# Two transformer blocks in one launch: a finer chain ahead of the experts, a reordered entry to block two, and turns of the identity in three pauses

## The chip, the cores and the metric

One core of a Trainium2 chip runs the whole kernel in one launch. The metric is the device time in microseconds (us), the median of three runs. PE is TensorE, DVE is VectorE, ACT is ScalarE, SP is the engine that issues the weight loads. All arithmetic is float32.

## The reference, cut to what matters

```python
x = x + gt1 * rmsnorm(y, g_post_mix)           # y = merged branches @ w_o, 256 tokens x 1024
h2 = rmsnorm(x, g_pre_ffn) * (1 + sc2) + sh2
logits = h2 @ w_router + b_router              # 32 experts
top_logits, top_e = lax.top_k(logits, 4)
top_w = softmax(top_logits)
gu = xe @ w_gu[e] + b_gu[e]                    # xe: the tokens of expert e
act = (clip(gu[:, D_FF:], -7, 7) + 1) * (min(gu[:, :D_FF], 7) * sigmoid(1.702 * ...))
yb = act @ w_dn[e] + b_dn[e]                   # added to the tokens, times top_w
x = x + gt2 * rmsnorm(f, g_post_ffn)           # f: the sum over a token's experts
# second block: h = rmsnorm(x, norm_mix_g_2); h @ w_in_2, gated linear attention, ...
```

## The kernel before, in words

The 256 tokens are two tiles of 128 (`tt`), each cut into two halves of 512 features (`h`); four such quarters make x. Each engine has one program written out by hand in the order in which it runs; semaphores (`wait_ge`, `then_inc`) join them. `step` on DVE waits until its own operation is done.

Weights stream through a ring of six slots of 2 MB. SP issues the load of a slot when PE has released it (`up_slot` for experts). An expert takes six slots, four for the up projection (`expert_item` on PE, L1830, products at L1839) and two for the down projection (L1876). For expert 0 the two down slots lie elsewhere (`first_down`), and slots 1, 2, 3 and then 0 are loaded during the merging and the `w_o` products; slot 0 last, once PE is done with the last `w_o` product. Expert 1's slots 4 and 5 are loaded ahead too, its slots 0 to 3 as PE releases them in item 0. From expert 2 on a loop loads each slot when the item before has released it. An item is an expert with up to 64 tokens; an expert with more has another item, with the same weights, for which nothing is loaded. There are 33 items here.

Ahead of the experts, for each tile: `w_o` products into PSUM banks `PB[0..3]` (`tokens`, L1551), ACT squares the halves and sums them (`square_half`, L742), DVE adds the two sums (`token_mean`, L1141), ACT takes the root (`token_root`, L748), DVE the reciprocal (`token_rstd`, L1147), scales the half with root and gain out of PSUM (`scale_y`, L1151) and adds it to x (`add_y`, L1156). ACT squares the new x, PE turns it (`turn_x`, L1733), ACT and for the last quarter DVE (L1185) copy the turned tiles, PE multiplies with the router weights (`router`, L1745), and DVE finds the four best experts (`top_experts`, L1163 to L1170). When both tiles are done PE makes ranks by a product with a triangle (L1765), DVE positions (L1190, L1192) and one hot matrices (L1198) of expert 0's tokens, PE gathers these tokens by a product with x (`gather`, L1807) and adds the up biases (`up_biases`, L1826), DVE copies the gathered rows (L1228), PE turns them (L1812), and DVE scales and shifts them (L1214, L1217) into `xe`, for which item 0's products at L1839 wait. During item 0 PE and DVE work out the overflow items (`overflow_counts`, `overflow_columns`), the first after slot 0, the second after slot 1.

After the last item PE adds the last outputs to the tokens (`combine`, L1818). Then ACT squares all four quarters, and DVE scales and adds (L1151, L1156), normalises for block two (`norm_half`, L1313), PE turns (`turn_normed`, L1908), ACT copies (L813), and PE starts block two with eight products of 512 columns for tile 0 (L1551), with the turns of tile 1 ahead of the seventh (`inside`). The low rank product (L1924) follows.

Of the kernel before, what the change touches and what calls it, by code (L numbers as in the profile page):

```python
# [24 lines left out]
P = 128  # L25
D = 1024
# [27 lines left out]
def layout(sizes):  # L54
# [10 lines left out]
    ("iota", P), ("cos", TT * DH), ("sin", TT * DH), ("carry", T), ("before32", NE), ("turn_id", 1), ("eps", 1),  # L65
# [11 lines left out]
def constants():  # L77
# [19 lines left out]
    put("iota", np.broadcast_to((p % CAP).astype(np.float32), (P, P)))  # L97
    nf = DH // 4
# [42 lines left out]
FOX_STEPS = 8  # L141


def two_blocks(nc, A, out):
    with ExitStack() as ctx:
# [272 lines left out]

        route_pe = sem("route_pe")
# [22 lines left out]
        moe_done = sem("moe_done")  # L442

# [144 lines left out]
        def _(act):  # L588
# [147 lines left out]
            def square_half(src):  # L736
# [5 lines left out]
                nc.scalar.activation([spare, spare_in, spare_mid, spare_final][0 if n < 8 else 1 if n < 16 else n // 4 - 2][n % 2], src, ACT.Square, scale=D ** -0.5, accum_out=part_ms[:, n:n + 1])\  # L742
                  .then_inc(part_sq, 1)

            def token_root(n):

                act.wait_ge(mean_ready, n + 1)
                nc.scalar.activation(tok_r[:, n:n + 1], mean_ms[:, n:n + 1], ACT.Sqrt, bias=C("eps"))\  # L748
                  .then_inc(tok_root, 1)
# [198 lines left out]
        def _(dve):  # L948
# [180 lines left out]
            V.memset(POSI, -FAR)  # L1129
# [8 lines left out]
            def token_mean(n):  # L1138

                dve.wait_ge(part_sq, 2 * n + 2)  # L1140
# [3 lines left out]
            def token_rstd(n):  # L1144

                dve.wait_ge(tok_root, n + 1)
# [12 lines left out]
            def top_experts(tt):  # L1159

                bank_ = [AS[1], AS[0]][tt]
                dve.wait_ge(logits_done, tt + 1)
                step(V.scalar_tensor_tensor(out=logit[:, tt, 0:NE], in0=bank_[:, 0:NE],  # L1163
# [6 lines left out]
                return V.tensor_tensor(sel[:, tt, :], mark[:, tt, 0:NE], logit[:, tt, 0:NE], ALU.is_gt)  # L1170

            dve.wait_ge(xtok_in, 16)
            dve.wait_ge(gain1_in, 16)
# [1020 lines left out]
```

## Time and profile before

| what | us |
|---|---|
| median of 3 runs (lowest, highest) | 1773.88 (1773.38, 1775.6) |
| the profiled execution's own time | 1777.78 |
| its span | 1776.0 |
| PE busy | 1685.5 (95%) |
| PE weight loads busy | 841.3 |
| DVE busy | 464.9 |
| ACT busy | 240.9 |
| products at L1839, 2112 of them | 472.1 |
| products at L1876, 1024 of them | 233.9 |
| expert loads, each 2 MB, 190 of them, issue to landing | 21.8 (median) |

The span is the profiled execution from its first to its last record; its own time holds what lies around it. Times in rows are from the start of the span. A busy PE is not PE at its peak. A row of the chain tells what the end of the program hung on at that time; PEclk is the granted TensorE clock as a share of 2.4 GHz.

### The profile page before, as it was taken

To read this page: it belongs to the slowest core of one execution; us is meant where nothing else is said; L and a number is where in the kernel's file an instruction comes from. 1 tells how busy PE (TensorE), PEld (TensorE's weight loads), DVE (VectorE), ACT (ScalarE), POOL (GpSimd) and SP (SyncE) were. 2 spreads that over 40 slices of the span, in tenths; PEclk is the share of its full clock that TensorE was granted. 3 is DMA by queue.
4 is the path that set the end of the run, shared out by engine and by line. 5 is a ranking of instruction groups with operands and counts; after the bars stand their busy time and mean duration, and the time that the engine had idled before them with its cause. 6 is when DMAs were issued, how large, how long until landed. Compare 5 with 4: busy or idle time off the path is not lost.

```text
span 1776.0 us, 19653 instructions
## 1 busy us (share of the span) xinstructions
PE 1685.5 (95%) x7790; PEld 841.3 (47%) x7791; DVE 464.9 (26%) x1031; ACT 240.9 (14%) x491; POOL 9.0 (1%) x5
## 2 busy tenths in 40 slices
PE   4999999899999999999999999999989999999998
PEld 2766677433333333332333333333344687588853
DVE  2303442421212212121212212121231623144411
ACT  2013440100000000000000000000131321100000
POOL 0010000000000000000000000000000000000000
PEclk9999999899999999999999999999989999999999
DMA  9652845569999999999799999999973232434400
GB/s 394 267 126 99 347 174 201 198 285 417 430 428 429 428 429 428 428 430 428 292 419 428 428 429 428 429 428 428 428 287 142 95 142 68 181 142 161 170 25 24
DMA packets 47841, 530.21 MB, mean 299 GB/s; under 512 B 13780, under 2 KB 13908, under 8 KB 15672
## 3 DMA queue, kind: packets, MB, share of 16 engines
q1 hardware_dynamic: 36720, 522.21, 71.0%
q10 hardware_dynamic: 11080, 7.42, 1.6%
q8 instruction: 30, 0.49, 0.1%
q14 instruction: 11, 0.09, 0.0%
HBM read 528.55 MB, written 1.06 MB: 298 GB/s over the span
## 4 chain that ended last, share of the span: by engine, by line
PE 71%; DMA 24%; DVE 3%; ACT 1%; issue 1%; SPq 0%; ACTq 0%; DVEq 0%
DMA ring<-experts_dram 23%; PE scores L1839 17%; PE proj L1551 10%; PE proj L2085 9%; PE att_out L1876 7%; PE proj L1541 6%; PE proj L2097 4%; PE proj L1668 3%; PE proj L1717 3%; PE turned L1807 2%; PE scores L1826 1%; PE scores L1633 1%; PE att_out L1657 1%; DMA rows<-rows_dram 1%; PE proj L1587 1%
## 5 line engine op out<-in xcount | busy, mean ns | idle before, releaser
L1839 PE MATMUL scores<-ring,arena 128*64 128x512 f32 x2112 | 472.1, 594 | 23.1 <-DMA ring<-experts_dram 19.8
L1839 PEld LDWEIGHTS scores<-ring,arena 128*64 128x64 f32 x2112 | 148.9, 137 | 333.1 <-issue 273.0
L1876 PE MATMUL att_out<-ring,arena 128*64 128x512 f32 x1024 | 233.9, 598 | 0.0
L1551 PE MATMUL proj<-ring,arena 128*128 128x512 f32 x384 | 170.1, 601 | 3.1 <-DVE arena L1116 2.5
L2085 PE MATMUL proj<-arena,ring 128*128 128x256 f32 x704 | 153.6, 382 | 0.7 <-ACT arena L813 0.7
L1290 DVE COPY arena<-turned 128x512 f32<-128x512 f32 x33 | 22.8, 692 | 480.4 <-PE turned L1807 480.4
L2085 PEld LDWEIGHTS proj<-arena,ring 128*128 128x128 f32 x704 | 134.7, 192 | 19.4 <-ACT arena L813 0.9
L1876 PEld LDWEIGHTS att_out<-ring,arena 128*64 128x64 f32 x1024 | 68.0, 136 | 140.9 <-issue 140.9
L1551 PEld LDWEIGHTS proj<-ring,arena 128*128 128x128 f32 x384 | 73.0, 192 | 92.1 <-issue 88.0
L1541 PE MATMUL proj<-arena,ring 128*128 128x256 f32 x512 | 113.1, 381 | 0.0
L1541 PEld LDWEIGHTS proj<-arena,ring 128*128 128x128 f32 x512 | 96.5, 190 | 14.9 <-issue 1.8
L793 ACT ACTIVATE arena<-arena 128x512 f32<-128x512 f32 x33 | 20.8, 629 | 556.1 <-DVE arena L1293 556.1
L2097 PE MATMUL proj<-ring,arena 128*128 128x512 f32 x176 | 75.7, 592 | 0.0
L1807 PE MATMUL turned<-xtok,arena 128*64 128x512 f32 x272 | 65.9, 606 | 0.7 <-DVE arena L1198 0.7
L1818 PE MATMUL proj<-arena 64*128 64x512 f32 x264 | 65.6, 615 | 0.8 <-ACT arena L802 0.8
L1204 DVE TENSOR_SCALAR arena<-cst,arena 128x128 f32<-128x128 f32 x68 | 20.5, 344 | 155.8 <-PE turned L1882 155.8
L1668 PE MATMUL proj<-arena,ring 128*128 128x256 f32 x256 | 59.5, 386 | 0.0
L1717 PE MATMUL proj<-arena,ring 128*128 128x256 f32 x256 | 55.8, 380 | 1.7 <-issue 1.0
L2097 PEld LDWEIGHTS proj<-ring,arena 128*128 128x128 f32 x176 | 33.4, 190 | 41.7 <-issue 41.6
L1717 PEld LDWEIGHTS proj<-arena,ring 128*128 128x128 f32 x256 | 48.5, 190 | 8.6 <-issue 1.2
L1668 PEld LDWEIGHTS proj<-arena,ring 128*128 128x128 f32 x256 | 47.3, 190 | 9.7 <-issue 3.9
L1293 DVE TENSOR_SCALAR arena<-scores 128x512 f32<-128x512 f32 x33 | 22.8, 692 | 90.4 <-PE scores L1839 90.4
(318 smaller groups left out, 1127.6 us busy)
## 6 DMA issues: line engine op xcount, KB each, us to landing
ring<-experts_dram SPq DMA_DIRECT2D x190, 2048.0 KB, 21.8
ring<-stream_dram SPq DMA_DIRECT2D x54, 2048.0 KB, 8.9
arena<-experts_dram SPq DMA_DIRECT2D x2, 2048.0 KB, 9.9
ring<-stream_dram SPq DMA_DIRECT2D x2, 1024.0 KB, 17.9
arena<-rpb_dram ACTq DMA_DIRECT2D x16, 128.0 KB, 4.3
arena<-gain_rows_dram ACTq DMA_DIRECT2D x3, 512.0 KB, 5.4
arena<-xT_dram SPq DMA_DIRECT2D x1, 1024.0 KB, 7.4
arena<-ctxT_dram SPq DMA_DIRECT2D x1, 1024.0 KB, 9.7
```

What stands on the lines that cost most here:

```text
L1290: V.tensor_copy(xg, PT[:, :]).then_inc(xg_ready, 1)
L1293: V.tensor_scalar(glu, AS[0][:, :], 7.0, None, ALU.min).then_inc(glu_ready, 1)
L1541: ins = mm(pb[:, c * T:c * T + T], W[:, k, (c0 + c) * P:(c0 + c) * P + P], src[:, k, :], start=k == 0, stop=k == K - 1)
L1551: ins = mm(pb[:, 0:n], src[:, k, tt * P:tt * P + P], W[:, k, 0:n], start=k == 0, stop=k == KD - 1)
L1668: ins = mm(PB[w % 2][:, 0:T], slot(n, KD, 512)[:, k, (w % 4) * P:(w % 4) * P + P], hT[:, k, :], start=k == 0, stop=k == KD - 1)
L1717: ins = mm(pb[:, c * T:c * T + T], slot(n, 4, D)[:, k, j * P:j * P + P], o[:, k, :], start=k == 0, stop=k == 3)
L1807: ins = mm(PT[parts, :], Sel[:, tt, :], xtok[:, tt, feats], start=tt == 0, stop=tt == TT - 1)
L1818: ins = mm(PB[2 * tt + h][:, :], SelWT[rows_, tile_of(tt)], yb[rows_, :], start=False, stop=False, skip_group_check=True)
L1839: ins = mm(AS[n][parts, :], xe[:, k % 4, k // 4, :], W[:, kk, n * D + feats.start:n * D + feats.stop], start=False, stop=k == KD - 1, skip ...
L1876: ins = mm(AO[parts, :], act_s[:, kk, s - 4, :], W[:, kk, feats], start=s == 4 and kk == 0, stop=s == 5 and kk == 3)
L2085: ins = mm(pb[:, c * T:c * T + T], W[:, k, c * 256 + j * P:c * 256 + j * P + P], hT[:, k, :], start=k == 0, stop=k == KD - 1)
L2097: ins = mm(PB[c][:, :], actT[:, 4 * n + k, tile_of(tt)], slot(DN0 + n, K, D)[:, k, half_of(h)], start=n == 0 and k == 0, stop=n == 5 and k ...
```

## The change

On the way to the experts: DVE multiplies a half of y with the gain while the root is not there yet, and a fused operation multiplies with the reciprocal and adds to x, in place of scale and add. The maxima are negated once for both tiles, after the one hots. `sel` of each tile is signalled by itself, the ranks of tile 0 are multiplied before `sel` of tile 1 is there, and a constant `iota_far` (128 columns more in `cst`) takes the offset of the positions, which are then one fused operation a tile. The gather of expert 0 works tile by tile into two banks with 256 columns each; DVE copies one and ACT the other, and `xe` is made in slices of 64 columns, half of them by ACT. Item 0's slot 0 waits for two of DVE's slices, slot 1 for ACT's, slot 2 for DVE's last. The up biases of item 0 stand ahead of the second router product, `overflow_counts` after slot 1 and `overflow_columns` after slot 2. The logits go to `PB[0]` and `PB[1]`, the ranks to `PB[2]` and `PB[3]`.

At the entry of block two: the same split into gain product and fused update, DVE and ACT taking tile 0's two banks in opposite order, tile 0's x squared and normed before tile 1's y is, and the first product waits for one copy instead of two. `PARTS` and `MEANS` give the new order of the sums.

`idle_turns` turns the identity matrix n times into a bank that nobody reads: 5 times after the first router product, 4 times between the rank products, 30 times after the last combine.

```diff
+    put("iota_far", np.broadcast_to((p % CAP + FAR + 1).astype(np.float32), (P, P)))
...
+PARTS = list(range(11)) + [12, 13, 11] + list(range(14, 24))
+MEANS = [0, 1, 2, 3, 4, 6, 5, 7, 8, 9, 10, 11]
...
-            act.wait_ge(top_ready, 1)
+            act.wait_ge(neg_max_ready, 1)
...
+            act.wait_ge(gathered, 1)
+            nc.scalar.activation(xg[:, 256:512], PB[0][:, 0:256], ACT.Copy).then_inc(xg_half, 1)
+            act.wait_ge(xg_t, 1)
+            for k in (2, 3, 6, 7):
+                ins = nc.scalar.activation(xe[:, k % 4, k // 4, :], PB[1][:, P * (k % 2) + CAP * (k // 4):][:, 0:CAP],
+                                           ACT.Identity, scale=A2[:, k:k + 1], bias=mod[:, 24 + k, 0:1])
+            ins.then_inc(xe_upper, 1)
...
-            for tt in range(TT):
-                act.wait_ge(moe_done, tt + 1)
-                for h in range(2):
-                    square_half(PB[2 * tt + h][:, :])
-                token_root(4 + tt)
-            for tt in range(TT):
-                square_of_x(4 + 2 * tt)
-                square_of_x(5 + 2 * tt)
-                token_root(6 + tt)
-                copy_normed(2 * tt, 0)
-                copy_normed(2 * tt + 1, 0)
+            act.wait_ge(moe_done, 1)
+            square_half(PB[0][:, :])
+            act.wait_ge(y_scaled, 1)
+            square_half(PB[1][:, :])
+            token_root(4)
+            act.wait_ge(moe_done, 2)
+            square_half(PB[2][:, :])
+            square_of_x(4)
+            square_of_x(5)
+            token_root(6)
+            square_half(PB[3][:, :])
+            copy_normed(0, 0)
+            copy_normed(1, 0)
+            token_root(5)
+            square_of_x(6)
+            square_of_x(7)
+            token_root(7)
+            copy_normed(2, 0)
+            copy_normed(3, 0)
...
-            def top_experts(tt):
...
+            def top_logits(tt):
...
-                step(V.scalar_tensor_tensor(out=logit[:, tt, 0:NE], in0=bank_[:, 0:NE],
+                step(V.scalar_tensor_tensor(out=logit[:, tt, 0:NE], in0=PB[tt][:, 0:NE],
...
-                V.tensor_scalar(nm1[:, tt:tt + 1], top8[:, tt, 0:1], -1.0, None, ALU.mult)
...
+            def top_experts(tt):
+                V.tensor_tensor(sel[:, tt, :], mark[:, tt, 0:NE], logit[:, tt, 0:NE], ALU.is_gt).then_inc(top_ready, 1)
+            def positions(tt):
+                dve.wait_ge(top_ready, tt + 1)
+                step(V.scalar_tensor_tensor(out=POSI[:, tt, 0:NE], in0=sel[:, tt, :], scalar=FAR,
+                                            in1=PB[2 + tt][:, 0:NE], op0=ALU.mult, op1=ALU.add))
+            def one_hot(tt, at):
+                return V.tensor_scalar(Sel[:, tt, :], C("iota_far")[:, 0:CAP], POSI[:, tt, at],
+                                       tok_r[:, 2 * tt + 1:2 * tt + 2], ALU.is_equal, ALU.mult)
...
+            expert_one_hot(slice(0, 1))
...
+                dve.wait_ge(part_sq, 4 * tt + 1)
+                V.tensor_tensor(scaled_mix[:, 0, :], PB[2 * tt][:, :], gain1[:, half_of(0)], ALU.mult)
                 token_mean(2 * tt)
+                step(V.tensor_tensor(scaled_mix[:, 1, :], PB[2 * tt + 1][:, :], gain1[:, half_of(1)], ALU.mult))
                 token_rstd(2 * tt)
...
-                    step(scale_y(tt, 2 * tt, gain1, h))
-                    add_y(tt, h, scaled_mix)
+                    V.scalar_tensor_tensor(out=xtok[:, tt, half_of(h)], in0=scaled_mix[:, h, :],
+                                           scalar=tok_r[:, 2 * tt:2 * tt + 1], in1=xtok[:, tt, half_of(h)],
+                                           op0=ALU.mult, op1=ALU.add).then_inc(x_half, 1)
                 if tt == 0:
+                    dve.wait_ge(x_half, 2)
                     token_mean(1)
                     token_rstd(1)
-            top_experts(0)
+            top_logits(0)
             dve.wait_ge(x_turned, 4)
...
+            top_experts(0)
             token_mean(3)
             token_rstd(3)
-            top_experts(1).then_inc(top_ready, 1)
-            dve.wait_ge(top_ready, 1)
-            step(V.tensor_scalar(mark[:, :, 0:NE], sel, FAR, -FAR - 1.0, ALU.mult, ALU.add))
+            top_logits(1)
+            top_experts(1)
+            dve.wait_ge(rank0_ready, 1)
+            positions(0)
+            one_hot(0, slice(0, 1)).then_inc(sel_first, 1)
             dve.wait_ge(route_pe, 1)
-            step(V.tensor_tensor(POSI[:, :, 0:NE], mark[:, :, 0:NE],
-                                 AS[1][:, 0:TT * NE].rearrange("p (t e) -> p t e", e=NE), ALU.add))
...
-                for tt in range(TT):
...
+            positions(1)
+            one_hot(1, slice(0, 1)).then_inc(sel_ready, 1)
+            V.tensor_scalar(nm1, top8[:, :, 0], -1.0, None, ALU.mult).then_inc(neg_max_ready, 1)
...
-            one_hots(slice(0, 1))
-            expert_one_hot(slice(0, 1))
+            dve.wait_ge(gathered, 1)
+            V.tensor_copy(xg[:, 0:256], PT[:, 0:256]).then_inc(xg_ready, 1)
+            dve.wait_ge(xg_half_t, 1)
+            for k in (0, 1, 4, 5):
+                ins = V.tensor_scalar(xe[:, k % 4, k // 4, :], AO[:, P * (k % 4) + CAP * (k // 4):][:, 0:CAP],
+                                      A2[:, k:k + 1], mod[:, 24 + k, 0:1], ALU.mult, ALU.add)
+                if k == 1:
+                    ins.then_inc(xe_lower, 1)
+            ins.then_inc(xe_ready, 1)
...
-            dve.wait_ge(gathered, 1)
-            V.tensor_copy(xg, PT[:, :]).then_inc(xg_ready, 1)
...
-            dve.wait_ge(xg_t, 1)
-            expert_input(step)
...
-                step(V.tensor_copy(n_e, PB[0][0:NE, 0:1]))
+                step(V.tensor_copy(n_e, PB[2][0:NE, 0:1]))
...
+            def gain_y(tt, h):
+                return V.tensor_tensor(scaled_ffn[:, h, :], PB[2 * tt + h][:, :], gain2[:, half_of(h)], ALU.mult)
+            def update_x(tt, h):
+                V.scalar_tensor_tensor(out=xtok[:, tt, half_of(h)], in0=scaled_ffn[:, h, :],
+                                       scalar=tok_r[:, 4 + tt:5 + tt], in1=xtok[:, tt, half_of(h)],
+                                       op0=ALU.mult, op1=ALU.add).then_inc(x_half, 1)
+            dve.wait_ge(moe_done, 1)
+            gain_y(0, 1).then_inc(y_scaled, 1)
+            dve.wait_ge(part_sq, 9)
+            step(gain_y(0, 0))
             token_mean(4)
             token_rstd(4)
-            step(scale_y(0, 4, gain2, 0))
-            token_mean(5)
-            add_y(0, 0)
-            step(scale_y(0, 4, gain2, 1))
-            add_y(0, 1)
-            token_rstd(5)
-            step(scale_y(1, 5, gain2, 0))
+            update_x(0, 0)
+            update_x(0, 1)
+            dve.wait_ge(x_half, 6)
+            dve.wait_ge(part_sq, 11)
+            gain_y(1, 0)
             token_mean(6)
-            step(scale_y(1, 5, gain2, 1))
             token_rstd(6)
...
-            for h in range(2):
-                add_y(1, h)
+            dve.wait_ge(part_sq, 14)
+            step(gain_y(1, 1))
+            token_mean(5)
+            token_rstd(5)
+            update_x(1, 0)
+            update_x(1, 1)
             token_mean(7)
             token_rstd(7)
...
             turn_x(1)
...
             router(0)
+            idle_turns(AS[0], 5)
             turn_x(2)
             turn_x(3)
+            pe.wait_ge(ohb_ready, 1)
+            pe.wait_ge(bgu_in, 48)
+            up_biases()
             router(1)
             pe.wait_ge(top_ready, 1)
-            for tt in range(TT):
-                for s in range(tt + 1):
-                    ins = mm(AS[1][:, tt * NE:tt * NE + NE], tri[:, s, tt * P:tt * P + P], sel[:, s, :],
-                             start=s == 0, stop=s == tt)
-            ins.then_inc(route_pe, 1)
-            mm(PB[0][0:NE, 0:1], sel[:, 0, :], ones[:, 0:1], start=True, stop=False).then_inc(up_slot, RING)
-            mm(PB[0][0:NE, 0:1], sel[:, 1, :], ones[:, 0:1], start=False, stop=True).then_inc(route_pe, 1)
+            mm(PB[2][:, 0:NE], tri[:, 0, 0:P], sel[:, 0, :], start=True, stop=True).then_inc(rank0_ready, 1)
+            mm(PB[3][:, 0:NE], tri[:, 0, P:2 * P], sel[:, 0, :], start=True, stop=False)
+            idle_turns(PB[0], 4)
+            pe.wait_ge(top_ready, 2)
+            mm(PB[3][:, 0:NE], tri[:, 1, P:2 * P], sel[:, 1, :], start=False, stop=True).then_inc(route_pe, 1)
...
-                mm(PB[0][0:NE, 1:2], C("before32")[0:NE, :], eblk[:, 2:3], start=True, stop=True).then_inc(route_pe, 1)
+                mm(PB[2][0:NE, 1:2], C("before32")[0:NE, :], eblk[:, 2:3], start=True, stop=True).then_inc(route_pe, 1)
...
-            halves = [(slice(CAP * b, CAP * b + CAP), slice(512 * b, 512 * b + 512)) for b in range(2)]
+            def gather_first(tt):
+                for q, bank_ in enumerate((PT, PB[0])):
+                    for parts, feats in halves:
+                        ins = mm(bank_[parts, 0:256], Sel[:, tt, :],
+                                 xtok[:, tt, feats.start + 256 * q:feats.start + 256 * q + 256], start=tt == 0,
+                                 stop=tt == TT - 1)
+                return ins
...
-                pe.wait_ge(xe_ready, i + 1)
+                if not first:
+                    pe.wait_ge(xe_ready, i + 1)
...
+                    if first and s == 0:
+                        pe.wait_ge(xe_lower, 1)
+                    if first and s == 1:
+                        pe.wait_ge(xe_upper, 1)
+                    if first and s == 2:
+                        pe.wait_ge(xe_ready, 1)
...
-                    if first and s == 0:
+                    if first and s == 1:
...
-                    if first and s == 1:
+                    if first and s == 2:
...
+            pe.wait_ge(sel_first, 1)
+            gather_first(0)
             pe.wait_ge(sel_ready, 1)
-            gather()
-            pe.wait_ge(ohb_ready, 1)
-            pe.wait_ge(bgu_in, 48)
-            up_biases()
-            pe.wait_ge(xg_ready, 1)
-            turn(AO, xg).then_inc(xg_t, 1)
+            gather_first(1).then_inc(gathered, 1)
+            mm(PB[2][0:NE, 0:1], sel[:, 0, :], ones[:, 0:1], start=True, stop=False).then_inc(up_slot, RING)
+            mm(PB[2][0:NE, 0:1], sel[:, 1, :], ones[:, 0:1], start=False, stop=True).then_inc(route_pe, 1)
+            for c in range(4):
+                if c == 0:
+                    pe.wait_ge(xg_ready, 1)
+                if c == 2:
+                    pe.wait_ge(xg_half, 1)
+                ins = nc.tensor.transpose([AO, PB[1]][c // 2][:, c % 2 * P:c % 2 * P + P], xg[:, c * P:c * P + P], ident)
+                if c == 1:
+                    ins.then_inc(xg_half_t, 1)
+            ins.then_inc(xg_t, 1)
...
+            idle_turns(AS[0], 30)
...
-            pe.wait_ge(hT_ready, 2)
+            pe.wait_ge(hT_ready, 1)
...
-            tokens(slot(0, KD, 512), hT, 0, inside=lambda: [turn_normed(hn1, c, 0) for c in (2, 3)])
+            tokens(slot(0, KD, 512), hT, 0, inside={4: lambda: pe.wait_ge(hT_ready, 2),
+                                                    6: lambda: [turn_normed(hn1, c, 0) for c in (2, 3)]})
...
+            def idle_turns(bank_, n):
+                for _ in range(n):
+                    nc.tensor.transpose(bank_[:, 0:P], ident, ident)
```

## Rows read from the trace of the kernel before

**Rows 1.** The page, part 2: busy tenths in 40 slices of the span.
```profile
PE   4999999899999999999999999999989999999998
...
DMA  9652845569999999999799999999973232434400
```

**Rows 2.** Chain that ended last, experts: start us, us, what.
```profile
379.26 10.30 PE scores L1839 x48
...
406.83 10.30 PE scores L1839 x48
...
582.94 25.48 DMA ring<-experts_dram
```

**Rows 3.** Windows before item 0: stretch, length, busy of each engine, PEclk, DMA share, GB/s.
```profile
330.00:332.00 2.00, 2.00 (x12) 2.00 (x11) 0.51 (x3) 1.59 (x3) 0.00 (x0) 0.50 0.31 131
...
334.00:336.00 2.00, 1.79 (x10) 1.65 (x10) 0.53 (x3) 0.53 (x2) 0.00 (x0) 0.50 0.00 0
```

**Rows 4.** Timeline of SP's queue after item 0's first slot: start us, us.
```profile
347.99 69.66 SPq L531 DMA_DIRECT2D ring<-experts_dram  x13
```

**Rows 5.** Windows, columns as in rows 3: the three stretches at the lower clock.
```profile
328.00:342.00 14.00, 11.55 (x46) 6.96 (x46) 6.62 (x31) 3.38 (x8) 0.00 (x0) 0.51 0.19 81
...
366.00:372.50 6.50, 6.50 (x21) 1.83 (x21) 0.76 (x2) 0.60 (x1) 0.00 (x0) 0.50 0.68 290
...
1298.00:1308.00 10.00, 7.08 (x14) 3.75 (x15) 5.76 (x13) 3.23 (x10) 0.00 (x0) 0.50 1.01 430
```

**Rows 6.** Timeline: start us, us, engine, line, operation, [idle before <-releaser], ahead of the experts.
```profile
323.81 1.87 PE L1745 MATMUL scores<-arena 128*128 128x32 f32 x16
...
324.79 0.16 DVE L1141 TENSOR_TENSOR small<-small 128x1 f32<-128x1 f32 x1 [9.52 <-ACT arena L742]
...
325.52 0.75 DVE L1151 SCALAR_TENSOR_TENSOR arena<-proj,small,arena 128x512 f32<-128x512 f32 x1
...
327.05 0.66 PE L1733 MATMUL turned<-cst,xtok 128*128 128x128 f32 x4 [1.38 <-DVE xtok L1156]
...
329.35 3.46 PE L1745 MATMUL scores<-arena 128*128 128x32 f32 x16
329.59 0.69 DVE L1185 COPY arena<-att_out 128x512 f32<-128x512 f32 x1
...
334.15 0.53 ACT L787 ACTIVATE arena<-arena,small 128x32 f32<-128x32 f32 x2 [1.96 <-DVE arena L1170]
...
334.17 1.49 PE L1765 MATMUL scores<-arena,cst 128*128 128x32 f32 x6 [1.36 <-DVE arena L1170]
...
336.62 3.68 PE L1807 MATMUL turned<-xtok,arena 128*64 128x512 f32 x8 [0.65 <-DVE arena L1198]
...
340.23 1.96 PE L1826 MATMUL scores<-arena 64*64 64x512 f32 x8
...
342.82 0.69 DVE L1214 TENSOR_TENSOR arena<-att_out,small 128x512 f32<-128x512 f32 x1 [1.27 <-PE att_out L1812]
...
344.29 3.65 PE L1839 MATMUL scores<-ring,arena 128*64 128x512 f32 x16 [1.51 <-DVE arena L1217]
...
357.36 1.89 PE L1807 MATMUL turned<-xtok,arena 128*64 128x512 f32 x8
```

**Rows 7.** Timeline, as rows 6: PE at the entry of block two.
```profile
1291.02 1.99 PE L1818 MATMUL proj<-arena 64*128 64x512 f32 x8 [0.79 <-ACT arena L802]
...
1300.23 1.11 PE L1908 MATMUL turned<-cst,arena 128*128 128x128 f32 x4 [7.23 <-DVE arena L1313]
...
1302.89 7.95 PE L1551 MATMUL proj<-ring,arena 128*128 128x512 f32 x12 [0.69 <-ACT arena L813]
...
1313.36 1.07 PE L1924 MATMUL turned<-arena 128*32 128x256 f32 x16
```

**Rows 8.** Chain that ended last, its first piece.
```profile
1.65 15.57 DMA rows<-rows_dram
```

**Rows 9.** DMA issues: what, queue, KB, us to landing.
```profile
cst<-cst_dram ACTq DMA_DIRECT2D x1, 849.5 KB, 7.6
```

More of the change, by code:

```diff
@@ L417, in two_blocks @@
         hT_ready = sem("normed_half_copied")
+        neg_max_ready = sem("negated_maxima_ready")
+        rank0_ready = sem("first_token_ranks_ready")
+        sel_first = sem("first_token_sel_ready")
+        xg_half = sem("gathered_upper_columns_copied")
+        xg_half_t = sem("gathered_lower_columns_turned")
+        xe_lower = sem("first_xe_lower_tiles_ready")
+        xe_upper = sem("first_xe_upper_tiles_ready")
         route_pe = sem("route_pe")
@@ L741, in square_half @@
                     act.wait_ge(part_sq, n - 1)
-                nc.scalar.activation([spare, spare_in, spare_mid, spare_final][0 if n < 8 else 1 if n < 16 else n // 4 - 2][n % 2], src, ACT.Square, scale=D ** -0.5, accum_out=part_ms[:, n:n + 1])\
+                scratch = [spare, spare_in, spare_mid, spare_final][0 if n < 8 else 1 if n < 16 else n // 4 - 2][n % 2]
+                nc.scalar.activation(scratch, src, ACT.Square, scale=D ** -0.5,
+                                     accum_out=part_ms[:, PARTS[n]:PARTS[n] + 1])\
                   .then_inc(part_sq, 1)
             def token_root(n):
-                act.wait_ge(mean_ready, n + 1)
+                act.wait_ge(mean_ready, MEANS.index(n) + 1)
                 nc.scalar.activation(tok_r[:, n:n + 1], mean_ms[:, n:n + 1], ACT.Sqrt, bias=C("eps"))\
@@ L1246, in overflow_items @@
                 lo, begin, end = eblk[:, 3:4], eblk[:, 4:5], eblk[:, 5:6]
-                step(V.tensor_tensor(lo, PB[0][0:NE, 1:2], C("turn_id")[0:NE, :], ALU.add))
+                step(V.tensor_tensor(lo, PB[2][0:NE, 1:2], C("turn_id")[0:NE, :], ALU.add))
                 step(V.tensor_tensor(begin, lo, ident[0:NE, 0:1], ALU.subtract))
@@ L1543, in features, with tokens @@
                 ins.then_inc(state[1], 1)
-            def tokens(W, src, tt, n=512, inside=None):
+            def tokens(W, src, tt, n=512, inside={}):
                 pb = bank()
                 for k in range(KD):
-                    if inside is not None and k == 6:
-                        inside()
+                    if k in inside:
+                        inside[k]()
                     ins = mm(pb[:, 0:n], src[:, k, tt * P:tt * P + P], W[:, k, 0:n], start=k == 0, stop=k == KD - 1)
@@ L1744, in router, with up_biases @@
                         pe.wait_ge(xT_ready_b, 1)
-                    ins = mm([AS[1], AS[0]][tt][:, 0:NE], hT[:, k, tile_of(tt)], wr2[:, k, :], start=k == 0,
+                    ins = mm(PB[tt][:, 0:NE], hT[:, k, tile_of(tt)], wr2[:, k, :], start=k == 0,
                              stop=k == KD - 1)
                 ins.then_inc(logits_done, 1)
+            halves = [(slice(CAP * b, CAP * b + CAP), slice(512 * b, 512 * b + 512)) for b in range(2)]
+            def up_biases():
+                for parts, feats in halves:
+                    for n in range(2):
+                        rows_ = slice(64 * n, 64 * n + 64)
+                        ins = mm(AS[n][parts, :], OHb[rows_, :], bgu[rows_, feats], start=True, stop=False,
+                                 skip_group_check=True)
+                ins.then_inc(bias_added, 1)
             pe.wait_ge(merged_ready, KD)
@@ L2073, in _ @@
             tokens(slot(12, KD, 512), merged2, 1)
-            tokens(slot(13, KD, 512), merged2, 1, inside=lambda: [turn_normed(hn2, c, 4) for c in (0, 1)])
+            tokens(slot(13, KD, 512), merged2, 1, inside={6: lambda: [turn_normed(hn2, c, 4) for c in (0, 1)]})
             turn_normed(hn2, 2, 4)
```

34 lines of the change are left out of this document (13 added, 21 removed).

## The prediction

> **What bounds the kernel now.** I read the page's forty slices first (44.4 us each), then the chain that ended last, then the timelines of the two stretches that the diff touches, then the granted clock. PE is busy in nearly every slice; DMA is full from the tenth to the twenty-ninth, about 400 to 1290 [rows 1]. The chain [rows 2] shows how the two take turns. An expert item costs PE 27.6 us (379.26 to 406.83). From 582.94 the chain goes over the load of expert weights: 25.48 us of DMA, then 3.7 to 3.9 of PE, about 29.4 us an item. So most of the span can't be shortened by PE or DVE. But a load is issued only when PE releases a ring slot, and the stream has no head start: the DMA engines are idle at 334 to 336 [rows 3], and SP issues expert 1's slot 0 at 347.99, just after PE has used slot 0 for the first time (344.29 plus 3.65) [rows 4, 6]. The whole stream of loads is hung on the start of the first item. What item 0 starts earlier, everything up to 1291 ends earlier, DMA bound or not.
>
> The path touched is thus (a) from the last `w_o` product (to 323.8) to item 0's first product at 344.29, and (b) from the last combine at 1291.02 to block two's first product at 1302.89 and on to 1313.36, where the low rank product starts. In both PE waits for DVE and ACT, and in both the granted clock falls to its lower level (1.2 of 2.4 GHz): 328 to 342 and 1298 to 1308, mean 0.51 and 0.50 [rows 5].
>
> **Part a, step by step.** *x update.* Before, after the square sum (324.79 plus 0.16) come root, reciprocal, a 0.75 us scale out of PSUM and an add, which at 512 columns is 0.69; PE turns the quarter at 327.05, in 0.66 [rows 6]. Now the gain product (0.7, by the same row) runs beside ACT's root, and one fused 0.7 us operation follows: 324.95 + 0.75 + 0.25 + 0.7 = 326.65, and the last quarter 0.7 later, 327.35, against 328.38. Gain 0.35 and 1.0. *Copy and second router.* DVE drops one operation and moves two, so its copy of 512 columns starts at 328.3 instead of 329.59 and ends at 329.0. PE fills the time with the four up bias products, off the path from now on. Router 1 starts at about 328.9; the second half's copy holds it little. It took 3.46 us with the clock low, router 0 took 1.87 with it high [rows 6]. End 330.8 (high) or 332.4 (low), against 332.81.
>
> *Ranks.* From the router's end (332.81) to the first use of `sel` (ACT, 334.15) it is 1.3 us [rows 6], now 1.2 with one operation fewer: `sel` at 332.0. PE has done all but one of the three rank products; each is 0.5 low (1.49 for three) or 0.25 high. Four turns take 0.43 at 0.11 each and end at 331.8, before `sel`. Last rank 332.35. Positions fall from two DVE operations and a wait to one fused one (0.22), and token half 0 has position and one hot while PE is at the rank: `sel_first` 332.6, `sel_ready` 333.2. *Gather.* 3.68 us low, 1.89 high for the same operation [rows 6]. Half 0 starts at 332.65; in all it ends at 334.4, against 340.3. *Copy, turns, input.* Before: up biases (1.96) and beside them the 0.69 copy, then turns, then two operations on 512 columns from 342.82, and the product at 344.29 [rows 6]. Now DVE and ACT copy 256 columns each (half of 0.69, with the fixed part 0.4), two turns, and DVE makes two 64 column slices (about 0.2 each) before PE may begin: 334.5 + 0.4 + 0.35 + 0.45 = 335.7, say 335.8. ACT's four slices, about 0.25 each, end by 336.6 and slot 1 wants them only at 339.2; ACT's exponentials before them (0.53 [rows 6]) end by 334.0. Total for (a): 344.3 - 335.8 = **8.5 us gained** with the clock high. New operations here have no row of their own; bounds from the nearest: a PSUM slice of 64 columns between 0.15 and 0.35, the same for ACT, so the start lies between 335.4 and 336.6.
>
> Cover. Expert 0's slot 0 must have landed: SP issues it when PE ends the last `w_o` product, and DMA moves its last bytes between 330 and 332 [rows 3]; 335.8 leaves 4 us. Item 0's inner work is the same; the expert counts and the overflow columns move one slot later in PE's order, which gives DVE 3.4 us more for each, so I cost them at nothing; if DVE were later than that, PE would stand in item 0 with slots landed.
>
> **The clock.** Part (a) costs at the low level: router +1.6, ranks +0.4, gather +1.8, turns +0.2, less 0.5 that hides beside DVE: 3.5 us. So with a low clock (a) gains 5.0. The five, four and thirty turns are there for this. At 5 x 0.11 the first fill 325.7 to 326.2, at no cost, since PE waits until 326.65.
>
> **Part b.** Before: the four squares and the two x updates in series; first normed half at 1300.2, turned, copied, product at 1302.89 after both copies [rows 7]. Now: square of half 0 from 1292.2, DVE takes half 1's gain product meanwhile, then half 0's; second square ends at 1293.6, mean, root, reciprocal 0.8: 1294.4; two fused 0.7: 1295.1, 1295.8; squares of x to 1296.7 (they now follow the updates directly, 0.7 apart); mean, root, reciprocal 0.75; normed half 0.75: PE turns at 1298.25 against 1300.23 [rows 7]. First product after one copy: 1298.25 + 0.45 + 0.65 = 1299.35 against 1302.89. Then six of eight steps (5.15 at 0.86 a step), the turns of the second token half, for which DVE is ready at 1304.5 and 1305.15 (0.3 late), 1.7 for the last two: 1307.3. The row of before for the same point is 1313.36. **Gain 6.0 us** with the clock high. Thirty turns are 3.3 us, 1293.0 to 1296.3, at no cost before 1298.25; at the low clock they would be 6.4 and late by 1. Weights of block two's slot 0 land before 1299 either way: the stream fills six slots in turn and its first has landed by the first product already today [rows 7]. With the clock low (b) loses 2.8 on the product (twelve records took 7.95 against 5.16) and 0.2 on turns: it gains 3.0.
>
> **Part c.** The constants grow by 128 columns, 64 KB on 849.5, on the ACT queue ahead of `rows`, with which the chain opens (15.57 us) [rows 8, 9]. At 131 to 430 GB/s, the rates in [rows 3, 5], this is 0.15 to 0.5; if the chain's opening waits for `rows` alone and its packets don't queue behind, 0. I take **0.3 lost**.
>
> **Does a turn of the identity hold the clock?** The trace cannot decide it: no stretch of before is filled by turns alone. It shows that it fell at 1298 after 5 us of nothing, at 328 after short pauses among turns and 32 column products, and that it stayed low from 1298 to 1308 although turns lay in it, from 1300.23 [rows 5, 7]. The last speaks a little against turns. The Trainium skill, TensorE: Matmul & The Clock Gate, Part 4: PE-mode transpose, says that the full clock doesn't engage for transposes, since they don't count as busy in the same way. By that rule this case would come out as the first rival; the trace agrees only in that the turns from 1300.23 didn't raise it.
>
> **Sum.** Against the profiled execution (span 1776.0, own time 1777.78): +0.3 - 8.5 - 6.0, and +1.0 since even held by turns the clock will fall in some executions: -13.2, 1764.6. The median of the runs is 3.9 below that execution, which gives 1760.7. Nothing shows what the 3.9 is; as part of it may be clock that the timed runs did not lose and can't win back, I add a third of it, 1.3: **1762.0 us**. A further low stretch, 366 to 372.5 in item 0, at mean 0.50 [rows 5], costs some 3 us of PE time; it begins in 32 row bias products that the diff leaves as they are, and may stay or go: 3 us either way in a single execution.
>
> **Rivals.** *Turns don't hold the clock.* +0.3 - 5.0 - 3.0 = -7.7: 1777.8 - 7.7 - 3.9 = **1766.2**. For it: turns that raised nothing. Against it: the pauses themselves get shorter. *Part (a) is swallowed by the expert stream*, only (b) stays: 1777.8 + 0.3 - 6.0 - 3.9 = **1768.2**. Against it: idle DMA before 348. *The edits do less than they say*, because the finer pieces each pay for their handing over: some 30 new waits at 0.1 and slices at 0.35 instead of 0.2 take 4 us, the clock another 7, **1770 to 1774**. *Slower:* the pauses in finer pieces let the clock fall late, near 334, and item 0, with its bias products of 32 rows, never raises it before item 1. Its some 30 us of PE work at half speed would cost 27: 1762 + 27 = **1789**; it decides from 12 us of PE work beyond today's at the low level. Against it: today the clock is low from 328 to 342 and no longer, at a longer pause [rows 5].
>
> **Chances.** Forecast 0.50; turns without effect 0.38; swallowed 0.05; less than said 0.04; slower 0.03. A measurement here tells 0.2% (3.5 us) from nothing. The first three are faster by more: 0.93; within 0.04; slower 0.03. The two likely cases with 3 us of item 0's clock and the slices' bounds reach from 1757.5 to 1768.5.
>
> **What would show it.** Item 0's first expert product at 335 to 337, and SP's load of expert 1 slot 0 3.7 us later; gather near 1.8 us; the granted clock 1.00 from 325 to 345 and from 1293 to 1310; item 1 again at 27.6 us and a 29.4 us rhythm in the DMA stretch, shifted as a whole; the low rank product 16.3 us after the last combine starts, against 22.3. Wrong if the clock is low in either stretch, if the first product waits for ACT's slices or a load, or if the shift at item 1 isn't found at 1291.

## The result, and the profile after

The changed kernel's median is 1762.95 us (6 runs, 1759.59 to 1766.7) against 1774.74 (6 runs, 1772.73 to 1778.85): 11.8 us faster, ratio 0.9931 (95% interval 0.9915 to 0.9946). (The three runs of the table above are among these six.) Its profiled execution took 1762.79, with a span of 1760.9. The page, part 2, for [rows 1]:

```profile
PE   4999999999999999999999999999999999999998
...
DMA  9642845779999999999799999999974232344400
```

Nothing is to be seen there: PE is at 90% or more in all slices but the first and the last; before, two more stood at 8. The change shows in the timeline, ahead of the experts, for [rows 6]:

```profile
325.30 1.87 PE L1816 MATMUL proj<-arena 128*128 128x32 f32 x16
...
327.01 0.74 PE L1744 MATMUL scores<-cst 128*128 128x128 f32 x5
327.02 0.16 DVE L1175 RECIPROCAL small<-small 128x1 f32<-128x1 f32 x1
327.22 1.42 DVE L1231 SCALAR_TENSOR_TENSOR xtok<-arena,small,xtok 128x512 f32<-128x512 f32 x2
...
328.02 0.66 PE L1804 MATMUL turned<-cst,xtok 128*128 128x128 f32 x4 [0.27 <-DVE xtok L1231]
...
329.27 1.09 PE L1826 MATMUL scores<-arena 64*64 64x512 f32 x8
...
330.29 1.97 PE L1816 MATMUL proj<-arena 128*128 128x32 f32 x16
...
333.56 0.41 PE L1852 MATMUL proj<-arena,cst 128*128 128x32 f32 x2 [0.38 <-DVE arena L1199]
...
334.01 0.65 PE L1888 MATMUL turned<-xtok,arena 128*64 128x256 f32 x4
...
336.96 1.10 DVE L1272 TENSOR_SCALAR arena<-att_out,small 128x64 f32<-128x64 f32 x4 [0.53 <-PE att_out L1984]
337.18 1.29 ACT L806 ACTIVATE arena<-proj,small 128x64 f32<-128x64 f32 x4 [0.79 <-PE proj L1984]
337.61 7.09 PE L1927 MATMUL scores<-ring,arena 128*64 128x512 f32 x32 [0.47 <-DVE arena L1272]
```

Router 1 takes 1.97 us where it took 3.46; the first expert product follows 12.31 us after router 0's start, where it took 20.48; slots 0 and 1 run in one piece of 7.09 without waiting for ACT's slices. SP issues expert 1's slot 0 at 341.31, 3.70 after that product's start, as before. The same for the entry of block two, PE alone, for [rows 7]:

```profile
1280.22 1.99 PE L1907 MATMUL proj<-arena 64*128 64x512 f32 x8 [0.79 <-ACT arena L822]
...
1282.14 3.49 PE L1744 MATMUL scores<-cst 128*128 128x128 f32 x30
...
1287.45 0.66 PE L2005 MATMUL turned<-cst,arena 128*128 128x128 f32 x4 [1.82 <-DVE arena L1364]
...
1288.80 5.42 PE L1617 MATMUL proj<-ring,arena 128*128 128x512 f32 x12
...
1296.74 1.07 PE L2022 MATMUL turned<-arena 128*32 128x256 f32 x16
```

Twelve records in 5.42 instead of 7.95. The windows over both places and over item 0 (stretch, length, busy of each engine, PEclk, DMA share, GB/s) answer to [rows 5]:

```profile
326.00:342.00 16.00, 14.52 (x104) 8.73 (x105) 10.32 (x45) 6.39 (x18) 0.00 (x0) 1.00 0.36 133
355.00:374.00 19.00, 19.00 (x88) 6.70 (x86) 5.38 (x12) 2.21 (x4) 0.00 (x0) 1.00 0.44 174
1280.00:1296.00 16.00, 13.93 (x69) 8.66 (x70) 9.64 (x21) 8.71 (x25) 0.00 (x0) 1.00 1.01 431
```

The clock is at its higher level throughout all three. The next table divides the profiled executions of both kernels and of the experiments by the starts of PE's records, in us. "Start" runs from the big modulation product near 42 us to router 0, "item 0" from its first product to item 1's first, "stream" from there to the last combine, "entry" on to the low rank product, "rest" to the end of the span:

| kernel | start | router 0 to first expert product | item 0 | stream | entry | rest |
|---|---|---|---|---|---|---|
| before | 281.76 | 20.48 | 34.80 | 911.93 | 22.34 | 462.64 |
| changed | 283.28 | 12.31 | 31.58 | 911.03 | 16.52 | 464.16 |
| no_turns | 283.02 | 13.64 | 33.16 | 911.67 | 19.11 | 464.18 |
| turns_only | 283.32 | 19.20 | 31.57 | 911.35 | 22.12 | 462.57 |
| entry_only | 282.94 | 19.02 | 31.57 | 911.54 | 16.52 | 463.82 |
| chain_only | 281.76 | 12.31 | 33.16 | 909.50 | 21.64 | 464.19 |
| long_turns | 281.83 | 13.72 | 34.80 | 911.76 | 36.31 | 464.38 |
| biases_back | 283.15 | 12.01 | 31.58 | 911.52 | 16.52 | 464.06 |
| more_turns | 280.27 | 12.31 | 31.57 | 910.56 | 16.52 | 461.24 |
| spread_more | 280.27 | 12.31 | 32.74 | 911.14 | 18.22 | 461.29 |
| spread_before | 281.81 | 20.50 | 32.74 | 910.84 | 22.22 | 464.18 |
| dve_alone | 281.70 | 12.30 | 33.16 | 912.55 | 18.21 | 464.19 |

From before to changed: 8.2 us in the chain, 3.2 in item 0, 0.9 in the stream, 5.8 at the entry; 1.5 and 1.5 are lost at the start and in the rest. Sum 15.1, the difference of the spans. (Products, and the changed kernel run once more, divide as the changed kernel does, within 0.3 us but for the stream, which is 0.6 shorter in the second.)

The profiled execution of before is one of its slower ones, so this overstates the change. turns_only below is the kernel before with turns that brought no time in its median; its profiled execution took 1773.97, near the median of before, and it is 3.9 us shorter than that of before: chain 1.3, item 0 3.2, stream 0.6, entry 0.2 shorter, start 1.6 longer. entry_only, with the old way to the experts and no turns there, shows the same start, chain and item 0 within 0.4. Against turns_only the changed kernel gains 6.9 in the chain and 5.6 at the entry and loses 1.6 in the rest. In these two executions the clock was low for longer at the start than in that of before (about 7 us after 40 instead of 3.5), for a shorter time ahead of the experts (10.2 instead of 13.7) and not at all in item 0. Why was not found.

### The profile page after: what moved, and what is told of

It reads as the page before. It is cut to its first block, busy times and chain, and to the rows that moved or that the text cites. A ratio compares the mean times of both kernels' runs of the same rounds, so it can differ in the third digit from the quotient of the medians.

```text
span 1760.9 us, 19760 instructions
## 1 busy us (share of the span) xinstructions
PE 1680.9 (95%) x7837; PEld 842.6 (48%) x7838; DVE 464.2 (26%) x1032; ACT 242.5 (14%) x496; POOL 9.0 (1%) x5
## 4 chain that ended last, share of the span: by engine, by line
PE 71%; DMA 24%; DVE 3%; issue 1%; ACT 1%; SPq 0%; ACTq 0%; DVEq 0%
DMA ring<-experts_dram 23%; PE scores L1927 17%; PE proj L1617 9%; PE proj L2183 9%; PE att_out L1964 7%; PE proj L1607 6%; PE proj L2195 4%; PE proj L1734 3%; PE proj L1788 3%; PE turned L1896 2%; PE scores L1826 1%; PE proj L1653 1%; PE scores L1699 1%; PE att_out L1723 1%; DMA rows<-rows_dram 1%
## 5 line engine op out<-in xcount | busy, mean ns | idle before, releaser
L1896 PE MATMUL turned<-xtok,arena 128*64 128x512 f32 x264 | 62.3, 592 | 0.0
L1256 DVE TENSOR_SCALAR arena<-cst,arena 128x128 f32<-128x128 f32 x68 | 20.5, 344 | 152.6 <-PE turned L1970 152.5
L1788 PEld LDWEIGHTS proj<-arena,ring 128*128 128x128 f32 x256 | 48.5, 190 | 8.6 <-issue 1.2
```

What stands on the lines that cost most here:

```text
L1788: ins = mm(pb[:, c * T:c * T + T], slot(n, 4, D)[:, k, j * P:j * P + P], o[:, k, :], start=k == 0, stop=k == 3)
L1896: ins = mm(PT[parts, :], Sel[:, tt, :], xtok[:, tt, feats], start=tt == 0, stop=tt == TT - 1)
```

## The experiments

**The three turns taken out (no_turns).** Its edit:

```diff
-            idle_turns(AS[0], 5)
-            idle_turns(PB[0], 4)
-            idle_turns(AS[0], 30)
```

> The changed kernel without its 39 turns of the identity; all else as in it. Theory A (the turns hold the clock): the granted clock falls in both pauses as before the change, so 5.0 instead of 8.5 us are gained ahead of the experts and 3.0 instead of 6.0 at the entry: some 5 to 6 us slower than the changed kernel, 1768 to 1769 us, and the low clock shows near 328 to 340 and near 1284 to 1297. Theory B (the shorter pauses alone keep the clock, turns do nothing): the time of the changed kernel, 1763 us, and the clock 1.00 in both places.

1767.96 us (1767.25 to 1769.52), ratio to before 0.9959 (0.9945 to 0.9973): 5.0 us slower than the changed kernel. Windows of no_turns:

```profile
334.00:337.40 3.40, 3.18 (x18) 1.64 (x15) 0.42 (x1) 0.91 (x3) 0.00 (x0) 0.51 0.00 0
1290.00:1296.60 6.60, 6.27 (x14) 3.48 (x15) 3.93 (x10) 3.06 (x8) 0.00 (x0) 0.51 1.01 429
```

The clock is low in both places. In the chain it fell only at 334 and cost 1.3 us (13.64 against 12.31), at the entry 2.6; another 1.6 lie in item 0, where it was low again. At the entry it was low after a pause of 5.24 us:

```profile
1290.33 1.11 PE L2002 MATMUL turned<-cst,arena 128*128 128x128 f32 x4 [5.24 <-DVE arena L1364]
```

One profile doesn't tell what the turns do in the chain: long_turns, which has them there, also has the clock low there, from 332.0 to 335.6, and takes 13.7 us too. But all five times of no_turns lie above all twelve of the changed kernel, 1767.25 and up against 1766.70 and down. So the 39 turns together are worth some 5 us.

**The kernel before with the turns alone (turns_only), and each part alone (entry_only, chain_only).**

> The kernel before with only the turns: 5 after the first router product, 4 before the rank products, 30 after the last combine. Theory A: where the turns hold the clock the low stretches of 13.7 and 10.2 us shorten; the pauses are as long as before (7.2 us at the entry, of which 3.3 are filled), so only a part comes back: 2 to 5 us faster than before. Theory B: no difference from before, and the clock low in the same two places.

1775.45 us, ratio 1.0005 (0.9994 to 1.0015): nothing. Its windows:

```profile
331.40:341.60 10.20, 8.86 (x34) 5.13 (x38) 4.05 (x21) 2.31 (x5) 0.00 (x0) 0.50 0.06 26
...
1297.40:1304.00 6.60, 5.91 (x10) 2.69 (x11) 2.86 (x7) 2.62 (x7) 0.00 (x0) 0.50 1.02 434
```

The low stretches are 10.2 and 6.6 us long instead of 13.7 and 10.2. For the chain this is no work of the turns: in entry_only, which has none there, the stretch is as short (from 329.8 to 340.2), and the chain is 19.02. At the entry PE is at work through 5.9 us of the low stretch, before through 7.2; what was removed lay mostly over a pause, and the entry is 0.2 shorter. After the thirty turns 3.8 us of pause remained, in the changed kernel 1.8:

```profile
1296.63 0.66 PE L1916 MATMUL turned<-cst,arena 128*128 128x128 f32 x4 [3.80 <-DVE arena L1313]
```

> The kernel before with the new entry to block two and its 30 turns; the way to the experts is the old one. From the last combine to the low rank product 16.5 us (in the changed kernel) instead of 22.3: 5.8 us faster than before, 1768 to 1769, if the two parts add up; item 0's first product 20.5 us after the start of the first router, as before. If one part's gain were swallowed, this or the run of the other part would show no gain.

1769.63 us, ratio 0.9975 (0.9963 to 0.9987), 5.0 us faster; entry 16.52 as expected. Item 0's first product came 19.0 us after router 0 and not 20.5: the old chain itself takes one or the other.

> The kernel before with the new way to the experts and its 5 and 4 turns; the entry to block two is the old one, without turns. From the first router to item 0's first product 12.3 us (in the changed kernel) instead of 20.5, and everything to the last combine earlier by that: 8 us faster than before, 1766 to 1767, and at the entry 22.3 us with the clock low as before. If the stream of expert loads swallowed it, the shift would be gone by the last combine and the time that of before.

1768.96 us, ratio 0.9964 (0.995 to 0.9977): 5.6 us faster, where 8 were expected. Its chain is 12.31, but the expectation reckoned from the 20.5 of one execution; against the 19.0 to 19.2 of the two others 6.7 to 6.9 can be gained, and in this execution the clock fell in item 0 (33.16). The parts' 5.0 and 5.6 add up to 10.6 of the 11.8, within their intervals. The stream takes 909.5 to 912.6 in all profiles, wherever it begins, so it swallows nothing.

**Do turns count? (long_turns, products)** In long_turns `idle_turns(AS[0], 30)` became 230.

> The changed kernel with 230 turns of the identity instead of 30 after the last combine, some 25 us of turns and nothing else on PE. Theory A (PE working on turns counts towards the clock): the granted clock stays 1.00 through them, a turn takes 0.11 us to its end, 24.6 us for all, and the first product of block two follows; the time is 22 us above the changed kernel's, 1785. Theory B (turns don't count): the clock falls within some us of their start as it fell 5 us after the last combine before the change, turns then take 0.21 each, 45 us or so in all, and the time is above 1800.

1786.77 us, a single execution, where theory A said 1785. The window and the timeline of long_turns:

```profile
1287.00:1311.00 24.00, 24.00 (x222) 24.00 (x221) 4.93 (x11) 3.13 (x10) 0.00 (x0) 1.00 0.74 314
```

```profile
1286.23 25.33 PE L1744 MATMUL scores<-cst 128*128 128x128 f32 x230
```

24 us with nothing but turns on PE, and the clock is at its higher level in all of it. In products the turn became `mm(bank_[:, 0:P], ident, ident, start=True, stop=True)`, 2, 2 and 15 of them.

> The changed kernel with full products of the identity in place of turns, two records each, half as many (2, 2 and 15), so that PE is occupied for about as long. Theory A: no difference, 1763 us, the clock 1.00 in both places. Theory B: products hold the clock where turns don't; since the changed kernel had it at 1.00 in its profile, B would then say that here it is so in more executions: 1 to 3 us faster, 1760 to 1762.

1762.89 us (1762.37 to 1764.52), and all segments as in the changed kernel. A turn serves as well as a product, within 1 us. Both tests speak for theory A: turns hold the clock where it is high. That they raise it where it is low neither test shows.

Nor do short fills hold it each time. Eight profiles have the new entry with its short fill and some 1.8 us of pause behind it. In two of them, spread_more and dve_alone, the clock is low there for some 3.5 us, from 1287.4 and from 1290.8, when PE had been at work again for 1.6 us. The twelve records then take 7.11 instead of 5.42, and the entry 18.2 instead of 16.5. From spread_more:

```profile
1280.51 3.50 PE L1572 MATMUL scores<-cst 128*128 128x128 f32 x30
...
1287.17 7.11 PE L1622 MATMUL proj<-ring,arena 128*128 128x512 f32 x12
```

**Single edits in the chain.** In biases_back the call of `up_biases()` with its two waits stands behind the gather.

> The changed kernel with the four up bias products of item 0 back behind the gather instead of ahead of the second router product. Theory A: they were moved from the path into a pause; beside them stands only the 0.4 us copy, so 0.6 us come back between gather and first expert product (12.3 us from router 0 to there become 12.9), and PE has a pause of 1.0 more ahead of router 1, in which the clock may fall: 1763.5 to 1765. Rival: the second router product is not bound by the copy but by PE; then it starts 1.0 earlier and nothing is lost, 1763.

1766.68 us (4 runs, 1762.48 to 1768.19). The profiled execution is the fastest of the four and its chain is 0.3 shorter than the changed kernel's, 12.01: router 1 starts right behind the turns, 4.1 us after router 0 instead of 5.0, and the products behind the gather, beside DVE's copy, cost 0.6. So the rival was right, no pause opens ahead of router 1, and the move takes no time off the path but adds 0.3. The three others took 1766 to 1768 with a mean granted clock of 0.991 to 0.993 against 0.995, and no profile tells where they were low. The interval, 0.994 to 0.9972, overlaps that of the changed kernel. Whether the move is worth anything for the clock stays open.

In dve_alone ACT's share of `xe` went back to DVE.

> The changed kernel with ACT's share of item 0's input given back to DVE: both 256 column copies and all eight slices on DVE, in the order copy, copy, slices 0 and 1, then 2, 3, then the rest. Theory A (the first product waits for two slices, the rest is hidden behind slots 0 and 1): the second copy, 0.4, goes in front of the slices, so gathered to first product 2.1 instead of 1.7 us, and slots 1 and 2 wait for nothing: 0.4 us slower, 1763.4, which the times won't show and the profile will. Rival (ACT's share carries the gain): slot 1 or 2 would wait, 1 us or more slower.

1763.21 us (4 runs, 1762.09 to 1766.13); gather's start to first product 3.60, as in the changed kernel. Timeline of dve_alone:

```profile
334.58 0.42 DVE L1262 COPY arena<-turned 128x256 f32<-128x256 f32 x1 [1.39 <-PE proj L1887]
334.92 0.41 DVE L1263 COPY arena<-proj 128x256 f32<-128x256 f32 x1
...
335.54 0.59 DVE L1269 TENSOR_SCALAR arena<-att_out,small 128x64 f32<-128x64 f32 x2 [0.20 <-PE att_out L1983]
...
336.19 7.09 PE L1926 MATMUL scores<-ring,arena 128*64 128x512 f32 x32 [0.35 <-DVE arena L1269]
```

The second copy fills the time of the first two turns. Not even the 0.4 us came, so ACT's share carries none of the gain. (The profiled execution is the slowest of the four: the clock was low in item 0 and at the entry.)

The other edits of the chain and those of the entry were only tested all together; how the 5.6 and the 5.0 us divide among them is not shown.

**Other pauses (more_turns, spread_more, spread_before).** more_turns adds `idle_turns(AS[0], 36)` behind the first modulation's turns and `idle_turns(AS[0], 26)` before the third turn of `hn2`.

> The changed kernel with turns in two more pauses, 36 in the 4.6 us pause behind the first modulation's turns (from 37.5 us), 26 in the 3.0 us pause of the second block's middle (from 1519), where the changed kernel's profile shows its clock low for 6.8 us each. Theory A: both low stretches go, each gives back half of its length or a little less: 4 to 6 us faster than the changed kernel, 1757 to 1759. Theory B: nothing, 1763.

1761.76 us (1757.16 to 1762.34), ratio 0.9925 (0.9911 to 0.9939). In its profiled execution, 1757.16, the clock is never low before the last product:

```profile
0.00:1752.00 1752.00, 1682.15 (x7899) 845.72 (x7900) 463.23 (x1032) 242.54 (x496) 9.04 (x5) 1.00 0.74 302
```

Start and rest are 3.0 and 2.9 us shorter, as theory A said. But the other four took 1760.6 to 1762.3 with a mean granted clock of 0.995 to 0.998, so they lost clock somewhere: the median gives 1.2 us and not 4 to 6, and the intervals of the two kernels overlap.

To take item 0's low stretch away its four products over 32 rows (a stationary operand with 32 rows) were spread:

```diff
+                        if first and s == 3 and kk == 0:
+                            down_bias(0, 0)
...
-                    down_biases()
+                    down_bias(0, 1)
+                    down_bias(1, 0)
...
+                        if first and s == 4 and kk == 1:
+                            down_bias(1, 1)
```

> The changed kernel itself, beside the next ones on one chip: 1763 us, between 1759 and 1767.

> The kernel with the turns in two more pauses (36 and 26), and item 0's four down bias products, which work on 32 rows only, no longer in one piece of 3.4 us: one inside slot 3, two in the old place, one inside slot 4. Their sum of PE time is the same, and by the waits of the changed kernel slot 4's first product comes 1 us earlier and its last as before. Theory A (this piece of 32 row products lets the clock fall in a third of the executions, for 3 or 7 us): the upper times go (kernel with more turns: 1757.2 to 1762.3), median 1757 to 1759, and no low stretch in the profile but at the end. Rival (the clock of item 0 depends on something else): 1760 to 1762, as with more turns alone.

> The kernel before with only that: its four down bias products of item 0 spread. Its times fall in two groups, 1772 to 1776 and 1777 to 1779, a third of them in the upper, and its profiled execution, of the upper one, had a low stretch of 6.8 us in item 0. Theory A: the upper group goes, all times within 1771 to 1775. Rival: the two groups stay, and what parts them is elsewhere, at the start or the end.

On one chip: the changed kernel 1762.59 (1761.29 to 1766.69), ratio 0.9935 (0.9922 to 0.9947); spread_more 1759.62 (1759.14 to 1763.15), ratio 0.9915 (0.9902 to 0.9928), the best of all and 3.0 us below the changed kernel, just over the 1757 to 1759 of theory A, though its clock was low at the entry; spread_before 1776.51 (1774.11 to 1777.32), ratio 1.0007 (0.9998 to 1.0016), where theory A said 1771 to 1775. Ten of its eleven times lie between 1775.9 and 1777.4, so two groups are no longer to be told apart, but the median did not fall.

Spreading costs 1.2 us in item 0 where the clock is high (32.74 against 31.57); the move had been costed at nothing. PE now waits 0.44 of it for `act_t`. It gives back where item 0 would be at 33.16 or 34.80. That these products let the clock fall in item 0 agrees with the two profiles in which they are spread (none low there), against five of the twelve others with an item 0 of 33 us or more; in these the clock fell during these products or within 0.4 us of their end. It is not the only condition: in the other seven the clock stayed high over the same products. And 1.2 us don't bring the faster times of before to 1776, so what parts its two groups stays open.

## Why the prediction was right

The forecast was 1762.0, the median is 1762.95, inside its range, and the likeliest case, turns that hold the clock, is the one that no_turns and long_turns show. The two places, and the clock in them, were the right mechanism; the sum comes this near partly by luck, as the last points say. Point by point:

- *What bounds.* Right. The stream moves as a whole with item 0: SP's first load of expert 1 comes 3.7 us after item 0's first product in both, an item of the DMA stretch takes 29.4 us in both, and the stream 911.93 and 911.03.
- *Part a.* Forecast 335.8 from 323.81, 12.0 us; measured 12.31. Its steps fall where they were put, from router 0's start: router 1 forecast 5.1, measured 4.99; last rank product 8.2 and 8.26; gather 8.85 and 8.71. The 0.3 lies behind the gather, where 3.60 stand against 3.15: two of DVE's slices take 0.59 and not 0.45, four of ACT's 1.29 (0.29 and 0.32 apiece, within the bounds of 0.15 to 0.35), and the rest lies in the copy and the turns. Router 1 waited for the biases ahead of it, which I had taken for filling only; biases_back shows 0.3 for that. The 8.5 gained were reckoned from a chain of 20.48, which before has in one sort of its executions; in the other it is 19.0 to 19.2, and the gain 6.7 to 6.9.
- *Part b.* Forecast 8.3 from the combine to the first product and 16.3 to the low rank product; measured 8.58 and 16.52. The thirty turns ended at 1285.6, 1.8 us before PE was wanted, at no cost, as forecast.
- *Part c.* Mis-sized: forecast 0.3, measured nothing. `rows` came 0.27 later, and so did the next two steps of the chain, but the fourth began where it did before. Chain of the changed kernel:

```profile
1.65 15.84 DMA rows<-rows_dram
17.73 1.81 ACT arena L620
19.67 9.41 PE scores L1574 x32
29.08 7.05 PE proj L1628 x64
```

  The sums of squares at L1574 took the delay up: 9.41 us instead of 9.71 (the product behind them began at 29.11 before). What paces them was not followed.
- *The clock.* The prices at the low level were forecast as 3.5 and 3.0, so that turns would be worth 4.2 us (1766.2 less 1762.0). They are worth 5.0 in the medians, but by other terms: 1.3 in the chain, 2.6 at the entry and 1.6 in item 0 by one profile of no_turns. The first price is too high, because with the shorter pauses of the new chain the clock fell only at 334, behind the router and the ranks. The doubt whether turns hold the clock was unfounded: long_turns has 24 us of turns alone at 1.00. The Trainium skill (TensorE: Matmul & The Clock Gate, Part 4: PE-mode transpose) says that the full clock doesn't engage for transposes; this trace doesn't agree. The turns from 1300.23 that "didn't raise it" are no test of that: they are short (1.1 us each) and followed 7.2 us in which PE stood idle. The +1.0 for executions in which the clock falls in spite of turns was rightly put in: long_turns has it low in the chain (1.4 us), spread_more and dve_alone at the entry (1.7 us).
- *What was not foreseen.* Longer low stretches at the start (42.0 to 48.5 at a mean of 0.53 instead of 0.76) and in the second block cost the profiled execution 1.5 each; neither place was edited and they differ from execution to execution. Item 0's 3 us "either way" came out at 3.2 gained, in step with the loss at the start.
- *The 3.9 us between profiled execution and median.* Explained in its size: turns_only's profile, which stands for a common execution of before, is shorter by just 3.9, by 1.3 in the chain and 3.2 in item 0 and others that nearly cancel. By this reading the 1.3 in the chain were clock that most timed runs did not lose and could not win back. Taking 1.3 of the gap off the gain was thus right in kind, but the third was a guess, and that it is the same number is luck. So is it that the sum ends within 1 us: the losses of 1.5 at the start and in the rest, item 0's 3.2 and the stream's 0.9 were in no term and largely cancel.

## What to carry to other kernels

Where a stream of loads is paced by the release of its buffers, time taken off ahead of its first consumer can arrive at the end undiminished, even when the stream is DMA bound: here it took 909.5 to 912.6 us wherever it began. Fill a pause of PE only after it has been shortened: here the fill alone, with 3.8 us of pause behind it at the entry, gave nothing, shorter pauses without it 6.6 us, and both 11.8. Take several profiled executions before a term of 3 us is believed: stretches of low clock in places that no edit touched moved single executions by as much, and a cost read from one slow execution (20.5 us of chain) overstates what can be gained.

## What the runs showed of the hardware

Turns of a 128x128 float32 tile keep the granted clock at its higher level as products do: 230 in 25.33 us, 0.11 each, clock 1.00. Thirty of them in a pause do so mostly, not always: in two of seven profiles of the new entry (spread_more, dve_alone) the clock fell for some 3.5 us, 1.6 us after PE had resumed work. The clock can also fall while PE is 100% busy: in item 0 of the kernel before it fell during products over 32 rows [rows 5], in seven other profiles it stayed high over the same products.
